# Five Strassen pairs in the second in-projection of a two-block kernel

## The reference

```python
h = x @ w_in                                   # 1024 x 1024 @ 1024 x 2368
x_q, x_kv, k_rope_raw, gate_a, u_pool, gate_b = jnp.split(h, splits, axis=-1)   # 512, 256, 64, 512, 512, 512
y_a = mla_branch(x_q, x_kv, k_rope_raw, positions, ...) * jax.nn.silu(gate_a)
y_b = pool_branch(u_pool, pool_w, pool_scale) * jax.nn.silu(gate_b)
mix = jnp.concatenate([y_a, y_b], axis=-1) @ w_out
x = layer_norm(alpha * x + mix, ln_g[layer], ln_b[layer])
# mla_branch: q = rms_norm_2(x_q, q_norm_g) @ w_uq, kv = rms_norm_2(x_kv, kv_norm_g) @ w_ukv,
#   rope on q_rope and k_rope_raw with cos and sin of the positions, then causal attention with 4 heads
# pool_branch: means over the last 2, 4, 8, 16 tokens minus the token, times pool_w, times pool_scale
```

## Time and profile before

| | |
|---|---|
| median of 3 runs | 1683.83 us (1683.56 to 1684.65) |
| profiled execution, its own time | 1683.6 us |
| its span in the trace | 1681.8 us |
| TensorE, VectorE, ScalarE, GpSimd busy | 1666.5, 1256.2, 795.6, 452.0 us |

### The profile page before, as it was taken

The page is one execution under the profiler, slowest core; times in us unless marked ns, Lnnn a source line. Parts: engine busy times, 40 slices in busy tenths (PEclk is TensorE's granted clock), DMA queues, the critical chain, the costliest instruction groups (busy, mean ns, idle before and its releaser), DMA issues.

```text
span 1681.8 us, 20879 instructions
## 1 busy us (share of the span) xinstructions
PE 1666.5 (99%) x7597; PEld 1373.9 (82%) x7597; DVE 1256.2 (75%) x1494; ACT 795.6 (47%) x1066; POOL 452.0 (27%) x270
## 2 busy tenths in 40 slices
PE   9999999999999999999999999999999999999998
PEld 7788788888787888888888888888888888788786
DVE  6478791369999888888888879889737936777654
ACT  5667741236854433444344444455332327566531
POOL 4223222100015654555454000005432442201000
PEclk9999999999999999999999999999999999999999
DMA  7111112053412232222322974762322221010351
GB/s 265 52 48 37 50 51 76 25 213 94 169 51 88 76 98 75 75 87 84 91 75 96 327 267 153 247 195 62 101 88 63 88 88 31 26 63 26 114 218 75
DMA packets 161098, 176.99 MB, mean 105 GB/s; under 512 B 13566, under 2 KB 114692, under 8 KB 161028
## 3 DMA queue, kind: packets, MB, share of 16 engines
q1 hardware_dynamic: 158708, 167.67, 30.7%
q10 hardware_dynamic: 2320, 8.39, 1.3%
HBM read 140.38 MB, written 35.65 MB: 105 GB/s over the span
## 4 chain that ended last, share of the span: by engine, by line
PE 93%; DVE 4%; ACT 1%; issue 1%; DMA 1%; DVEq 0%; SPq 0%; ACTq 0%
PE ps L962 31%; PE ps L2603 27%; PE ps L2557 19%; PE ps L2849 5%; PE ps L2834 3%; PE ps L2499 1%; PE ps L2685 1%; PE ps L2888 1%; PE ps L2806 1%; DVE pt_lo L2376 1%; PE ps L2523 1%; DVE prob L2333 1%; PE ps L2822 1%; DMA x_tok<-in_x 1%; ACT pt_hi L1646 0%
## 5 line engine op out<-in xcount | busy, mean ns | idle before, releaser
L985 POOL TENSOR_TENSOR w_lo<-w_raw,w_hi 128x1024 fp32r<-128x1024 f32 x52 | 138.0, 2654 | 594.1 <-ACT w_hi L1097 592.3
L2603 PE MATMUL ps<-hop_hi_P,wop_hi_P 128*128 128x512 f32 x672 | 263.6, 392 | 2.0 <-DVE u L1974 0.8
L2603 PE MATMUL ps<-hop_lo_P,wop_hi_P 128*128 128x512 f32 x672 | 262.9, 391 | 0.0
L2603 PE MATMUL ps<-hop_hi_P,wop_lo_P 128*128 128x512 f32 x672 | 262.8, 391 | 0.0
L991 POOL TENSOR_TENSOR wop_lo_P<-pair_sum,wop_hi_P 128x512 fp32r<-128x512 f32 x90 | 137.3, 1526 | 351.5 <-ACT wop_hi_P L1108 351.5
L962 PE MATMUL ps<-h_hi,w_hi 128*128 128x512 f32 x688 | 214.1, 392 | 0.0
L962 PE MATMUL ps<-h_lo,w_hi 128*128 128x512 f32 x688 | 211.9, 389 | 0.0
L962 PE MATMUL ps<-h_hi,w_lo 128*128 128x512 f32 x688 | 211.8, 389 | 0.0
L962 PEld LDWEIGHTS ps<-h_hi,w_hi 128*128 128x128 f32 x688 | 128.2, 188 | 30.0 <-issue 4.3
L2603 PEld LDWEIGHTS ps<-hop_hi_P,wop_hi_P 128*128 128x128 f32 x672 | 126.9, 189 | 30.5 <-DVE u L1974 1.6
L962 PEld LDWEIGHTS ps<-h_lo,w_hi 128*128 128x128 f32 x688 | 129.1, 188 | 27.1
(11 more groups left out here) (386 smaller groups left out, 3403.8 us busy)
## 6 DMA issues: line engine op xcount, KB each, us to landing
pair_raw<-in_w_up SPq DMA_DIRECT2D x48, 512.0 KB, 4.9
w_raw<-in_w_in SPq DMA_DIRECT2D x46, 512.0 KB, 3.9
dn_raw<-gu_park SPq DMA_DIRECT2D x84, 256.0 KB, 3.9
dn_raw<-in_w_down SPq DMA_DIRECT2D x60, 256.0 KB, 3.1
gu_park<-up_cv SPq DMA_DIRECT2D x24, 512.0 KB, 2.6
out_raw<-in_w_out SPq DMA_DIRECT2D x30, 256.0 KB, 2.8
x_tok<-in_x SPq DMA_DIRECT2D x4, 1024.0 KB, 8.1
x_park<-xs SPq DMA_DIRECT2D x1, 4096.0 KB, 13.2
```

The costliest lines, as they stand in the source:

```text
L985: nc.gpsimd.tensor_tensor(lo[:, :], raw[:, :], hi[:, :].bitcast(f32), ALU.subtract).then_inc(w_lo_done, 1)
L2603: mm = nc.tensor.matmul(dst, w[q][:, k, :], x[q][:, k, :], start=a, stop=b, skip_group_check=True)
```

## The change

The ten latent and gate blocks become five pairs by the same scheme (three latent pairs, two of them of q, then two gate pairs), after the pool blocks and kr. What comes with it:

- The eight pool blocks go first, the transposes into ps3 stand between and inside them, then kr, whose scaled tile goes to HBM (kr_park) and comes back.
- The token operands of P5, P7, P6 and P4 are differences and sums of quarters of x: VectorE makes them (`mix_sum`), ScalarE casts them (`mix_high`), VectorE takes the remainders (`mix_low`), all beside the pool blocks.
- Weights of a pair: two loads of 512 KB (in_raw0, in_raw1), four sums on VectorE (in_sum), seven casts on ScalarE (in_hi), seven remainders on GpSimd (in_lo).
- The rope tables are made from a quarter of the columns (128x256) at a time, written to HBM in full form (trig_park) and loaded back when the pairs are done; the sign is applied in `rotate`.
- The tanh of the first pool gate stands ahead of the pooled cast; the reciprocals are cut in halves and stand, with the norms of the q tiles, in and behind the third pair's turn of VectorE.
- The positions for the masks are loaded and cast later, ahead of the first value tile.

The core of the diff:

```diff
@@ SyncE
+            for n in range(IN_PAIRS):
+                if n == 0:
+                    sp.wait_ge(block_done, N_KR)
+                for f in range(2):
+                    if n >= 1:
+                        sp.wait_ge(pair_sum_done, 4 * PAIRS + 4 * n)
+                        sp.wait_ge(wop_lo_done, in_made(("P2", "P4")[f], n - 1))
+                    sp.dma_start(in_raw[f][:, :, :], w2_v[:, :, IN_COLS[n][f]:IN_COLS[n][f] + P]).then_inc(pair_in[f], 16)
+            sp.wait_ge(wop_lo_done, in_made("P3", IN_PAIRS - 1))
+            sp.wait_ge(product, in_run("P5", IN_PAIRS - 1))
             uq = w_uq_2.rearrange("(k p) (h n) -> p k h n", p=P, h=HEADS)
...
+            nope_load(0)
+            sp.wait_ge(product, in_run("P7", IN_PAIRS - 1))
+            sp.wait_ge(bd_in, 64 + 9 * 16)
+            sp.dma_start(kr_raw[:, :], kr_park[:, :]).then_inc(pos_in, 16)
+            for i, t in enumerate((sin_t, cos_t)):
+                sp.dma_start(t[:, :], trig_park[i]).then_inc(pos_in, 16)
+            nope_load(1)
@@ ScalarE
+            for n in range(-1, IN_PAIRS):
+                last = n + 1 == IN_PAIRS
+                if not last:
+                    in_high("P7", n + 1)
+                    in_first_sum(n + 1)
+                if not last:
+                    in_high("P4", n + 1)
+                if n == 3:
+                    for i in range(Q_TILES):
+                        latent_high(i)
+                if 0 <= n < 3:
+                    latent_square(PAIR_LATS[n][1])
+                elif n >= 3:
+                    gate_tanh2(2 * n - 5)
+                if not last:
+                    in_high("P3", n + 1)
+                if n == 4:
+                    act.wait_ge(pos_in, POS_BACK)
+                    act.wait_ge(sums_done, in_sums("C22", n))
+                    swap_halves(0, kr_raw)
+                    act.wait_ge(gate_parked[1], GATE + 16)
+                    high(N_UQ + 1)
...
+                if n == 3:
+                    act.wait_ge(wop_lo_done, in_made("P3", IN_PAIRS - 1))
+                    high(N_UQ)
@@ VectorE
+            for n in range(IN_PAIRS):
+                in_third_sums(n)
+                if n == 2:
+                    latent_factor(0, T1)
+                elif n == 3:
+                    latent_normed(3)
+                    for t in (T1, T2):
+                        latent_factor(1, t)
+                    in_second_sum(4)
+                elif n == 4:
+                    latent_low(2)
+                    gate2(1)
+                    gate2(0)
+                in_result(n, 1)
...
+                in_result(n, 0)
+                if n + 2 < IN_PAIRS:
+                    in_second_sum(n + 1)
+                if n == 2:
+                    latent_factor(0, T2)
...
+                if n + 2 < IN_PAIRS:
+                    in_weight_sums(n + 2)
+                if n == 2:
+                    for i in range(3):
+                        latent_normed(i)
@@ TensorE
-            for i in range(2, Q_TILES + KV_TILES):
-                if i >= 4:
-                    pe.wait_ge(lat_done, i - 1)
-                project(N_IN2 + i, 0, ps[i % 2], h_hi, h_lo)
...
-            for h in range(HEADS):
...
-                project(N_GATE + h, 0, ps[h % 2], h_hi, h_lo)
+            block_with(N_POOL + 2, ps[0], lambda: (pe.wait_ge(final_gain, 16), pe.wait_ge(gb_done, 1), by_token(0)))
+            by_token(1)
+            pe.wait_ge(rstd3_spread, 1)
+            block_with(N_POOL + 3, ps[1], lambda: (by_token(2), pool_product(0)))
...
+            def in_product(q, n):
...
+                pe.wait_ge(wop_lo_done, in_made(q, n))
+                dst = in_bank(n, IN_BANK[q])
+                for k in range(4):
+                    x_hi, x_lo = ix_parts(q, slice(k, k + 1))
+                    for w, x, a, b in ((in_hi[q], x_hi, q in ("P1", "P6", "P5") and k == 0, False), (in_hi[q], x_lo, False, False),
+                                       (in_lo[q], x_hi, False, k == 3)):
+                        mm = nc.tensor.matmul(dst, w[:, k, :], x[:, 0, :], start=a, stop=b, skip_group_check=True)
+                mm.then_inc(product, 1)
+
+            for q, n in IN_ORDER:
+                in_product(q, n)
```

More of the change, by code:

```diff
@@ new lines, in program @@
+        acc_kv = tile("acc_kv", W0, 4)
+        square2 = tile("square2", S0, 4)
+        pw_raw = at("pw_raw", G0, [4, P])
+        pw_hi = at("pw_hi", G0 + 2048, [P], f32r)
+        pw_lo = at("pw_lo", G0 + 2560, [P], f32r)
+        pooled_hi = tile("pooled_hi", G0, 1, f32r)
+        pooled_lo = tile("pooled_lo", G0, 2, f32r)
+        y_pool = tile("y_pool", G0, 3, f32, 2)
+        tok_out = [tile(f"tok_out{s}", G0, n) for s, n in enumerate((5, 7))]
+        kr_out = tile("kr_out", G0, 5)
+        rstd3 = tile("rstd3", G0, 6)
@@ L1066, in _ @@
+            pool.wait_ge(latn_done, Q_TILES + KV_TILES)
+            low(N_UQ + 1)
+            low(N_UQ + 2)
+            latent_low(5)
+            for n in range(N_UQ + 3, N_BLOCKS):
+                low(n)
             pool.wait_ge(block_done, N_BLOCKS - 1)
@@ new lines, in latent_high @@
+            def latent_high(i):
+                act.wait_ge(latn_done, i + 1)
+                if i == 0:
+                    act.wait_ge(product, in_run("P6", IN_PAIRS - 1))
+                elif i == Q_TILES:
+                    act.wait_ge(ga_scaled, HEADS)
+                    act.wait_ge(gate_parked[1], GATE + 16 * HEADS // 2)
+                nc.scalar.copy(latents()[i][0], lat_tile(i)).then_inc(latn_hi, 1)
+            next_high(N_POOL + 2)
+            next_high(N_POOL + 3)
+            pool_tanh(0)
@@ new lines, in gate2, with latent_factor @@
+            def gate2(h):
+                dve.wait_ge(ga_th, GATES.index(h) + 1)
+                V.scalar_tensor_tensor(out=gate_out[h][:, :], in0=gate_out[h][:, :], scalar=1.0, in1=in_bank(3 + h // 2, h % 2),
+                                       op0=ALU.add, op1=ALU.mult).then_inc(ga_done, 1)
+            def latent_factor(which, t):
+                dve.wait_ge(root2_done, which + 1)
+                factor = (acc_q, acc_kv)[which]
+                V.reciprocal(factor[:, t], factor[:, t]).then_inc(rstd2_done, 1)
@@ new lines, in _ @@
+            pooled_gate(1)
+            pool_gate(2, "P6")
+            mix_sum("P4")
+            mix_low("P7")
+            mix_low("P6")
+            pooled(3)
+            pool_weight(3)
+            pooled_gate(2)
+            pool_gate(3)
+            in_weight_sums(0)
+            pooled_gate(3)
+            mix_low("P4")
+            for parked in res_parked:
+                dve.wait_ge(parked, 16 * NT // 2)
+            dve.wait_ge(block_done, read(N_KR))
+            V.tensor_tensor(kr_out[:, :], ps[0][:, :], rstd3[:, :], ALU.mult).then_inc(kr_scaled, 1)
@@ L2286, in rotate @@
+                step(V.scalar_tensor_tensor(out=sw[:, :], in0=sw[:, :], scalar=sign[:, 0:1], in1=sin_t[:, :],
+                                            op0=ALU.mult, op1=ALU.mult))
                 dve.wait_ge(rope_a, r + 1)
+                if r == 1:
+                    for parked in gate_parked:
+                        dve.wait_ge(parked, GATE + 16 * HEADS // 2)
                 V.tensor_tensor(scr[2][:, :], scr[0][:, :], sw[:, :], ALU.add).then_inc(rope_v, 1)
+                if r == 0:
+                    gate2(2)
+                elif r == 2:
+                    latent_low(4)
```

729 lines of the change are left out of this document (493 added, 236 removed).

## The result

The changed kernel takes 1690.6 us (1689.83 to 1691.89, five runs), the kernel before beside it 1684.13 us. The ratio is 1.0038, 95% interval 1.0024 to 1.0053: slower, where 1676.4 was forecast. It lies outside the range of 1671 to 1682.

The account below looks back on a forecast made before the run. TensorE was taken to bound the kernel, busy in 99% of the span. From 1683.6, minus 13.6 for matmuls gives 1670.0; plus waits of 1.1, 2.2, 2.6 and 0.5 gives 1676.4 us, range 1671 to 1682.

Parts of the forecast that it names:

- The matmuls: Ten blocks become five pairs: 60 fewer matmuls on TensorE at 0.2267 us each, 13.6 us less.
- Pairs at their matmul count: In the five new pairs no engine is full, so each runs at 84 matmuls, 19.04 us, without waits in the middle.
- rival C: GpSimd's turn-taking with VectorE sets the pairs' period, 22.9 against 19.04 us, making the kernel slower, 1695; chance 0.05.
- Edge 1: At the start, TensorE's first transposes wait 1.1 us for the first pool gate, through a VectorE collision with GpSimd; bounds 0 and 1.6.
- Edge 2: Reciprocal and norms in the third pair's turn delay U3, so the fourth pair's P4 waits 2.2 us; bounds 0 and 3.5.
- Edge 3: At the hand-over to the query weights, the rope weights' load comes late and TensorE waits 2.6 us; bounds 1.4 and 4.5.
- Behind the edges: After the hand-over, returning tables and later VectorE and ScalarE work cost 0.5 us in all; bounds 0 and 2.5.
- land about 19.5: The kr tile and both rope tables, issued from about 11.6 us after the last P6, land about 19.5 after it.
- rival B: Three 512 KB table loads land 4 us later, each microsecond going to TensorE; about 1680.5 us; chance 0.15.
- The clock: Read as 2.4 GHz throughout the span; no term for a fall of the clock in the sum.

Follow-up runs that it names:

- e5: The changed kernel with the three norms of the third pair moved behind the third sums of the fourth pair on VectorE; 1688.58 us.
- e1: The changed kernel with the rope query-weights load issued without waiting for the remainder of the last pair's P3; 1683.61 us.
- e8: The changed kernel with query heads 0 and 1's banks emptied before the second rotation and key latents done between the swaps; 1686.09 us.
- e9: The changed kernel with 18 matmuls that nothing reads ahead of query head 3's second product, before the third long wait; 1689.5 us.
- e3: The changed kernel with 16 and 15 matmuls that nothing reads in place of TensorE's first two long waits; 1691.79 us.
- e7: The changed kernel with the edits of e1, e8 and e5, plus an earlier gate product and an earlier first query swap; 1676.76 us.
- e2: The changed kernel with the three table loads and their two waits put ahead of the first query-weight load; 1683.81 us.
- e4: The changed kernel with a gate's parking and key-latent roundings and remainders moved ahead of work that needs the tables; 1691.24 us.

## Why the prediction was wrong, step by step

**The matmuls** (-13.6) were right: 60 fewer, at 0.2267.

**Pairs at their matmul count**: right. No wait in the middle of a pair shows; rival C did not occur.

**Edge 1** (1.1): 0.8. The collision came, but at the small step behind the pooling (2.24 us, 1183.42) instead of at the pooling step itself (1.22).

**Edge 2** (2.2): 1.3. The three norms took 6.77 against 7.4 charged (3.5 + 3.9), U3 ended 13.8 behind the start of U2 and not 14.8. e5 confirms that these norms make the wait. All four weight sums read two SBUF operands, not two of them as the prediction says; here none met GpSimd (2.66 us for the four).

**Edge 3** (2.6): 3.7. Nearly all of the difference is one term, GpSimd's remainder for P3: 2.37 instead of 1.30. VectorE takes the remainder of a q tile at 1364.45, within 0.01 us of it:

```profile
1359.72 2.41 POOL L1202 TENSOR_TENSOR qn_lo<-lat,qn_hi 128x1024 fp32r<-128x1024 f32 x1 [5.59 <-ACT qn_hi L1795]
1364.46 2.36 POOL L1187 TENSOR_TENSOR in_lo_P<-in_sum,in_hi_P 128x512 fp32r<-128x512 f32 x1 [2.33 <-ACT in_hi_P L1743]
1366.78 2.41 POOL L1202 TENSOR_TENSOR qn_lo<-lat,qn_hi 128x1024 fp32r<-128x1024 f32 x1
```

The same operation takes 1.30 in the earlier trace rows. The turn-taking that I charged at edge 2 belonged into this term as well, and I left it out. The three edges together are 5.8 for 5.9 forecast; that is luck, since each is off by 0.3 to 1.1.

**Behind the edges** (0.5, at most 2.5): this is the step that failed. Measured 3.5 + 4.1, and the clock. Two faults in it, and e1 with e8 separate them.

First, "land about 19.5" behind P6: 23.2. The first of the three issues began 12.4 behind P6 and not 11.6 (edge 3's term), the third at 13.4, and the last table took 9.8 us behind its issue, with three loads, two parked gates and query weights under way together. The lateness of 3.7 is about rival B's 4 us, and late tables are its mechanism, though no run separates the loads' row from the parked gates. But B was priced as one wait of 4 us for TensorE, and the tables feed a chain and not a wait: swap, rotation, gate, first swap of the queries, second swap.

Second, "VectorE and ScalarE then run some 3 us later against TensorE than before, and the first query remainder lands about when TensorE needs its bank". I never laid this chain out. Had I added its rows I would have found VectorE's rotations meeting GpSimd's remainders four times:

```profile
1385.18 1.28 DVE L2702 SCALAR_TENSOR_TENSOR scr<-scr,sign,sin_t 128x1024 f32<-128x1024 f32 x1 [3.07 <-ACT scr L1684]
1386.50 3.32 DVE L2708 TENSOR_TENSOR scr<-scr,scr 128x1024 f32<-128x1024 f32 x1
...
1396.68 3.39 DVE L2702 SCALAR_TENSOR_TENSOR scr<-scr,sign,sin_t 128x1024 f32<-128x1024 f32 x1
...
1407.16 2.18 DVE L2702 SCALAR_TENSOR_TENSOR scr<-scr,sign,sin_t 128x1024 f32<-128x1024 f32 x1
1409.38 3.40 DVE L2708 TENSOR_TENSOR scr<-scr,scr 128x1024 f32<-128x1024 f32 x1
...
1417.47 2.36 DVE L2725 TENSOR_TENSOR qh_lo<-ps,qh_hi 128x1024 fp32r<-128x1024 f32 x2
```

These operations take 1.23 to 1.28 alone. Some 7 us of the 33.7 from 1385.18 to 1418.84 are turn-taking with GpSimd (2.1 + 2.1 + 0.9 + 2.2). No run takes the turn-taking away by itself; these are differences between rows. And the order by which two engines empty the banks, harmless while they were ahead, decides now: e8 takes the third wait away with the same instructions. That chain was there in the kernel before (its UKV part begins at once behind the query block), with 32.6 us from the end of the rope block to work in. I had no row of how much of it was spare. The trace of before has one, and it says 1.4 us:

```profile
1411.93 2.36 DVE L2300 TENSOR_TENSOR qh_lo<-ps,qh_hi 128x1024 fp32r<-128x1024 f32 x2
```

In the changed kernel the UKV part starts 1.37 behind the start of that operation (1417.47 to 1418.84). By the same step it could have started at 1413.3 before, and TensorE came at 1414.74. From the first swap to there it was 29.9 us (from 1383.43), with one collision, of 1.4 us; in the changed kernel it is 38.0, with four.

In the prediction's own terms, P6 to the UKV part was 46.2 + 2.6 + 0.5 = 49.3 us; it was 61.2. The 11.9 between them, less the 1.2 that edges 1 and 2 were charged too much, is 10.7 of the 14.2 by which the time was missed. The clock behind the start of the UKV part is 1.8 more. Of the rest 0.8 lies between the profiled execution's own time (1689.8) and the median, 0.3 around the span (2.1 instead of 1.8), and 0.6 I can't place.

**The clock**: not in the prediction's sum at all. It reads the level of 2.4 GHz "throughout" and prices every wait at its length. Of the 5.7 us in TensorE's bill only what stands behind the third wait counts, 1.9, of which 1.6 is the clock (e9), because the first two falls lie inside the chain's 61.2 (e3 for the first, e9 for the second).

So the forecast was right about TensorE's work and wrong about what TensorE would wait for. e7 has the gain of the work and takes 1676.8. That this lies near the predicted 1676.4 is no credit to the prediction: it is another order of the work.

## What to carry to other kernels

When work is taken off the engine that bounds, every other engine's deadlines come closer by as much. List the chains that ran beside it (here from the last P6: remainder, issue, landing, swap, rotation, bank) and lay out each to its end with the durations it has under contention; an unlisted chain of 61.2 us beside 46.2 us of matmuls ate the 13.6 and more. Early issue of a load that many steps hang on is worth more than its own wait: 7 us for moving one wait of 3.7. And a wait of TensorE that ends a chain has two prices, its length and the clock behind it; one inside a chain has none of its own.

## What the runs showed of the hardware

**The clock falls behind some waits and not others, and length alone doesn't decide.** It fell to 1.2 GHz behind waits of 3.7, 3.5 and 4.1 us in the changed kernel, of 5.7 in e1, of 4.7 and 2.8 in e2, of 2.7 in e5 and of 2.6 in e3. Behind the waits of 0.6 to 1.6 that I looked at it did not, nor behind those of 3.6 in e8 and 3.4 in e9, at the same place in the program as the 3.5. For e9 the granted clock behind that wait:

```profile
1393.44:1398.44 5.00, 5.00 (x22) 4.14 (x23) 1.61 (x2) 4.65 (x5) 0.00 (x0) 1.00 0.50 176
```

Ahead of it TensorE had done the same block of 48 matmuls as in the changed kernel, but slower: 13.5 us in e8 and e9, where the changed kernel took 12.8, with more of them at 1.2 GHz. What decides stays open.

**A fall has no fixed price.** 48 matmuls behind a wait without one took 11.13 us (e9) and 11.15 (e4), with one 12.64 (e5), 12.77 (the changed kernel) and 13.66 (e1).

**Two engines with two SBUF operands each.** In the overlaps shown GpSimd's 128x512 remainder grows from 1.30 to 2.37, and VectorE's 128x1024 operations from 1.23 or 1.28 to between 2.2 and 3.4. The one that started first kept its time: VectorE took 1.22 from 1364.45 while GpSimd, 0.01 behind it, took 2.36, and GpSimd took 2.37 from 1386.37 while VectorE, 0.13 behind it, took 3.32. The Trainium skill, page SBUF — State Buffer, section "SBUF: two separate sides", has this exclusion; the trace agrees. Here it is some 7 us of a critical chain of 61.2.

**A load of the same size landed after 6 or after 10 us.** The 512 KB of cos_t, the third in a row each time, took 6.1 us to land in e1 and 5.9 in e2, 9.8 in the changed kernel, and 10.6 and 10.7 in e3 and e9. In the last three the other loads and two parked gates were issued close around it; which of them costs the 4 us isn't separated.
